# Expert pairs written out one after the other, token splits ahead of the weight splits at each joint, and twelve filler products

## What is computed

```python
def moe_swiglu(h, w_router, w_gate, w_up, w_down):
    logits = (h @ w_router).astype(jnp.float32)
    top_val, top_idx = lax.top_k(logits, TOP_K)
    top_w = jax.nn.softmax(top_val, axis=-1)
    gates = jnp.sum(jax.nn.one_hot(top_idx, N_EXPERTS, dtype=jnp.float32) * top_w[..., None], axis=-2)
    out = jnp.zeros_like(h)
    for e in range(N_EXPERTS):
        out = out + gates[..., e:e + 1] * swiglu(h, w_gate[e], w_up[e], w_down[e])
    return out
```

## Time and profile before

| | |
|---|---|
| median of 3 runs (lowest, highest) | 1273.4 us (1270.49, 1274.1) |
| the profiled execution's own time | 1276.08 us |
| its span in the profile | 1274.2 us, 16146 instructions |
| TensorE products, weight loads | busy 1221.2 us (96%), 854.6 us (67%) |
| VectorE, ScalarE, GpSimd | 689.5 us (54%), 539.2 us (42%), 106.9 us (8%) |
| mean granted TensorE clock | 0.985 of full |
| first products of the a-phases after joints 1 to 3 | at 601.01, 822.44 and 1044.35 us |
| moved by DMA | 412.58 MB, mean 324 GB/s |

### The profile page before, as it was taken

How to read it: one execution, slowest core, us unless ns; L and a number is a source line. 1 busy time by engine, 2 the same in 40 slices (tenths; PEclk the granted TensorE clock), 3 DMA queues, 4 the chain that set the end, 5 groups by cost and what they waited for, 6 DMA issues and landing times.

```text
span 1274.2 us, 16146 instructions
## 1 busy us (share of the span) xinstructions
PE 1221.2 (96%) x6044; PEld 854.6 (67%) x6044; DVE 689.5 (54%) x783; ACT 539.2 (42%) x522; POOL 106.9 (8%) x118
## 2 busy tenths in 40 slices
PE   9999999989989999998899999889999988999996
PEld 7888887778877888334688833568883346888332
DVE  3844445656578888102688710268861026886102
ACT  2643444455445776002577500257750025775001
POOL 0000000000003050100005010000501000050100
PEclk8999999999999999999999999999999999999998
DMA  9755553853266999999999999999999999999995
GB/s 314 257 187 178 196 178 120 199 188 131 100 248 225 372 363 360 347 409 414 413 415 406 368 371 408 415 414 415 407 346 386 407 415 414 415 406 341 391 407 209
DMA packets 141294, 412.58 MB, mean 324 GB/s; under 512 B 9683, under 2 KB 29139, under 8 KB 141142
## 3 DMA queue, kind: packets, MB, share of 16 engines
q1 hardware_dynamic: 140406, 408.23, 84.5%
q0 software_dynamic: 816, 3.28, 0.8%
HBM read 410.44 MB, written 1.05 MB: 323 GB/s over the span
## 4 chain that ended last, share of the span: by engine, by line
PE 85%; DMA 5%; DVE 3%; SPq 3%; issue 3%; ACT 1%; DVEq 0%; ACTq 0%
PE bank L1395 19%; PE bank L1396 19%; PE bank L1397 19%; PE bank L1768 13%; DMA raw<-in_moe_w_gate 4%; PE bank L1781 4%; SPq L545 3%; PE bank L1721 1%; PE bank L1402 1%; PE bank L1844 1%; PE bank L1491 1%; PE bank L1798 1%; PE bank L1657 1%; DMA head_row<-in_heads 1%; ACT w_hi L604 1%
## 5 line engine op out<-in xcount | busy, mean ns | idle before, releaser
L906 DVE TENSOR_TENSOR raw_lo<-raw,w_hi 128x2048 fp32r<-128x2048 f32 x149 | 339.8, 2300 | 101.4 <-ACT w_hi L604 101.2
L604 ACT ACTIVATE w_hi<-raw 128x2048 fp32r<-128x2048 f32 x149 | 284.5, 1916 | 148.3 <-PE bank L1397 95.7
L1395 PE MATMUL bank<-w_hi,h_hi 128*128 128x512 f32 x568 | 230.2, 405 | 19.4 <-DVE h_lo L1249 9.8
L1396 PE MATMUL bank<-raw_lo,h_hi 128*128 128x512 f32 x576 | 229.9, 399 | 9.1 <-issue 9.1
L1397 PE MATMUL bank<-w_hi,h_lo 128*128 128x512 f32 x568 | 226.5, 399 | 0.0
L1395 PEld LDWEIGHTS bank<-w_hi,h_hi 128*128 128x128 f32 x568 | 109.6, 193 | 50.2 <-DVE raw_lo L906 17.2
L1768 PE MATMUL bank<-raw,h_b 128*64 128x512 f32 (+1 forms) x768 | 143.1, 524 | 0.0
L1396 PEld LDWEIGHTS bank<-raw_lo,h_hi 128*128 128x128 f32 x576 | 111.1, 193 | 33.1 <-issue 10.4
L1397 PEld LDWEIGHTS bank<-w_hi,h_lo 128*128 128x128 f32 x568 | 109.2, 192 | 23.9
L906 DVE TENSOR_TENSOR raw_extra_lo<-raw_extra,w_hi 128x2048 fp32r<-128x2048 f32 x48 | 111.4, 2348 | 15.4 <-ACT w_hi L604 15.4
L1768 PEld LDWEIGHTS bank<-raw,h_b 128*64 128x64 f32 x768 | 53.7, 137 | 82.6 <-issue 74.5
(11 more groups left out here) (311 smaller groups left out, 1601.9 us busy)
## 6 DMA issues: line engine op xcount, KB each, us to landing
raw<-in_moe_w_gate SPq DMA_DIRECT2D x96, 1024.0 KB, 11.4
raw<-in_moe_w_up SPq DMA_DIRECT2D x80, 1024.0 KB, 11.8
raw<-in_moe_w_down SPq DMA_DIRECT2D x64, 1024.0 KB, 12.6
raw_extra<-in_moe_w_down SPq DMA_DIRECT2D x48, 1024.0 KB, 13.9
raw_extra<-in_moe_w_up SPq DMA_DIRECT2D x32, 1024.0 KB, 12.7
raw_extra<-in_moe_w_gate SPq DMA_DIRECT2D x16, 1024.0 KB, 7.4
raw<-in_ffn_w_gate SPq DMA_DIRECT2D x11, 1024.0 KB, 5.1
raw<-in_ffn_w_up SPq DMA_DIRECT2D x11, 1024.0 KB, 5.1
```

The source lines that it names most:

```text
L604: nc.scalar.activation(to, raw_slot(source), ACT.Copy).then_inc(hi_ready, 1)
L906: nc.vector.tensor_tensor(lo_slot(source), raw_slot(source), high.bitcast(f32), ALU.subtract).then_inc(lo_ready, 1)
L1395: mm(out, a_hi, b_hi, start=first, stop=False)
L1396: mm(out, a_hi, b_lo, start=False, stop=False)
```

## The change

1. Every engine but SyncE and GpSimd has the first four pairs written out in its program. A loop over further pairs follows, behind an `If` that skips it when there are only four. Inside the first three pairs the `If`s on the number of pairs are gone. The number of pairs is read in the fourth pair instead of before the first.
2. At the joint, `he_hi` stands ahead of `hi_e(ROUND_UNITS)` on ScalarE, and `he_lo` ahead of `lo_e(ROUND_UNITS)` on VectorE.
3. Ahead of the next expert's first unit TensorE runs twelve products of the identity with itself (`keep_warm(WARM[8])`, L1402).
4. The places `gpos` are computed by GpSimd in 13 chained steps instead of by VectorE; VectorE only copies `rank` out of PSUM for it. The order of the experts is made by VectorE after the first `aT_low` of pair 0 instead of before the pair.

```diff
-WARM = (16, 6, 10, 8, 28, 8, 8, 8)
+WARM = (16, 6, 10, 8, 28, 8, 8, 8, 12)
...
+def pair_follows(eng, p, pairs):
+
+    return nullcontext() if isinstance(p, int) and p < PAIRS - 1 else eng.If(pairs[0] > p + 1)
+
+
+def pair_count(eng, rtab_i):
+
+    return eng.value_load(rtab_i[0:1, 0:1], min_val=PAIRS, max_val=PAIRS + X_PAIRS)
...
-            sc.wait_ge(pairs_done, 1)
-            pairs = sc.value_load(rtab_i[0:1, 0:1], min_val=PAIRS, max_val=PAIRS + X_PAIRS)
-            with sc.Fori(0, pairs) as p:
+            pairs = [None]
+
+            def pair(p):
...
-                with sc.If(p < pairs - 1):
+                if is_pair(p, PAIRS - 1):
+                    sc.wait_ge(pairs_done, 1)
+                    pairs[0] = pair_count(sc, rtab_i)
+                with pair_follows(sc, p, pairs):
+                    he_hi(p, 1)
                     hi_e(ROUND_UNITS)
-                    he_hi(p, 1)
                     hi_e(ROUND_UNITS + 1)
...
+            for p in range(PAIRS):
+                pair(p)
+            with sc.If(pairs[0] > PAIRS):
+                with sc.Fori(PAIRS, pairs[0]) as p:
+                    pair(p)
...
             he_lo(0, halves=[1])
+            nc.vector.tensor_copy(rank[:, :, :], rank_ps).then_inc(rank_copied, 1)
             lo(MOE_U0 + 2)
             lo(MOE_U0 + 3)
 
-            link(nc.vector.tensor_tensor(more, incl, big, ALU.subtract))
...
-            nc.vector.reduce_sum(gpos[:, :, :], prod[:, :, :, :], AX.X).then_inc(gpos_done, 1)
...
+            def order_table():
+                nc.vector.max(order[:, :], key)
...
+                    if is_pair(p, 0) and s == 0:
+                        order_table()
...
-                with ve.If(p < pairs - 1):
+                with pair_follows(ve, p, pairs):
+                    he_lo(p, 1)
                     lo_e(ROUND_UNITS)
-                    he_lo(p, 1)
                     lo_e(ROUND_UNITS + 1)
                     lo_e(ROUND_UNITS + 2)
                     ve.wait_ge(acc_done, p * 8 + 6)
                     accumulate(p * 8 + 4)
...
-            pe.wait_ge(pairs_done, 1)
-            pairs = pe.value_load(rtab_i[0:1, 0:1], min_val=PAIRS, max_val=PAIRS + X_PAIRS)
-            with pe.Fori(0, pairs) as p:
+            pairs = [None]
+
+            def pair(p):
...
-                with pe.If(p < pairs - 1):
+                with pair_follows(pe, p, pairs):
                     pe.wait_ge(silu_done, q0 + ELEMENTWISE)
+                    keep_warm(WARM[8])
                     expert_in(p, ROUND_UNITS + j_gate(0), 0, gate_bank, range(2), p * 2 + 3)
...
+            for p in range(PAIRS):
+                pair(p)
+            with pe.If(pairs[0] > PAIRS):
+                with pe.Fori(PAIRS, pairs[0]) as p:
+                    pair(p)
...
-            po.wait_ge(gpos_done, 1)
+            base, cap, big, incl, more, shift, most = (ctab[:, i, :] for i in (4, 5, 6, 7, 8, 9, 10))
+            po.wait_ge(pairs_done, 1)
+            nc.gpsimd.tensor_tensor(more, incl, big, ALU.subtract).then_inc(pool_step, 1)
+            po.wait_ge(pool_step, 1)
...
+            po.wait_ge(pool_step, 12)
+            nc.gpsimd.tensor_tensor(gpos[:, :, :], prod[:, :, :, 0], prod[:, :, :, 1], ALU.add).then_inc(pool_step, 1)
+            po.wait_ge(pool_step, TABLE_STEPS)
```

More of the change, by code:

```diff
@@ L1 @@
-from contextlib import ExitStack
+from contextlib import ExitStack, nullcontext
 import numpy as np
@@ L53 @@
 LAST_YG = 10
-FIRST_STEPS = 9
+TABLE_STEPS = 13
+FIRST_STEPS = TABLE_STEPS + 9
 WHOLE_UNITS = 3
@@ L301, in trunk @@
         pairs_done = sem("pairs_done")
-        gpos_done = sem("gpos_done")
+        rank_copied = sem("rank_copied")
         sel_done = sem("sel_done")
@@ L1278, in _ @@
[L1278 to L1285, removed]
@@ L1294, in _ @@
[L1294 to L1299, removed]
@@ L1301, in _ @@
-            ve.wait_ge(pairs_done, 1)
-            pairs = ve.value_load(rtab_i[0:1, 0:1], min_val=PAIRS, max_val=PAIRS + X_PAIRS)
-            with ve.Fori(0, pairs) as p:
+            def order_table():
+                nc.vector.max(order[:, :], key)
+                link(nc.vector.tensor_tensor(within[:, :, :], incl[0:1, None, :].to_broadcast([1, X_PAIRS, E]),
+                                             iota[0:1, 0:X_PAIRS, None].to_broadcast([1, X_PAIRS, E]), ALU.is_le))
+                nc.vector.max_index(order_i[:, :], order[:, :], key)
+                link(nc.vector.reduce_sum(rtab[:, :], within[:, :, :], AX.X))
+                nc.vector.tensor_copy(rtab_i[:, 1:1 + PAIRS], order_i[0:1, 0:PAIRS])
+                nc.vector.tensor_scalar(rtab_i[:, 1 + PAIRS:1 + PAIRS + X_PAIRS], rtab[:, :], float(E - 1), None, ALU.min)
+                nc.vector.tensor_copy(rtab_i[:, 1 + PAIRS + X_PAIRS:1 + 2 * PAIRS + X_PAIRS],
+                                      order_i[0:1, PAIRS:2 * PAIRS]).then_inc(rtab_done, 1)
@@ L1366, in _ @@
                     accumulate(p * 8 + 4)
-                with ve.If(p < pairs - 1):
+                with pair_follows(ve, p, pairs):
                     lo_e(ROUND_UNITS + 3)
+            for p in range(PAIRS):
+                pair(p)
+            with ve.If(pairs[0] > PAIRS):
+                with ve.Fori(PAIRS, pairs[0]) as p:
+                    pair(p)
             assert yg[0] == LAST_YG
@@ L1853, in act_transposed, with old_sums @@
                     step.then_inc(aT_psum, 1)
-                for s in range(N_BG - 1):
[L1856 to L1862, removed]
+                def old_sums():
+                    pe.wait_ge(gT_done, p * 2 + 2)
+                    for tb in range(TB):
+                        for half in range(2):
+                            cols = slice(half * HALF, (half + 1) * HALF)
+                            mm(last_out(tb, half), ident, y[:, tb, cols], start=True, stop=False)
+                if is_pair(p, PAIRS - 1):
+                    pe.wait_ge(pairs_done, 1)
+                    pairs[0] = pair_count(pe, rtab_i)
+                for s in range(N_BG - 1):
+                    if s == N_BG - 2 and pairs[0] is not None:
+                        with pe.If(pairs[0] < p + 2):
+                            old_sums()
                     pe.wait_ge(silu_done, q0 + (N_EG + s + 1))
@@ L1888, in _ @@
                                start=True, stop=True).then_inc(sc_psum, 1)
-            pe.wait_ge(ye_act, pairs * 2)
-            pe.wait_ge(gT_done, pairs * 2)
+            for p in range(PAIRS):
+                pair(p)
+            with pe.If(pairs[0] > PAIRS):
+                with pe.Fori(PAIRS, pairs[0]) as p:
+                    pair(p)
+            pe.wait_ge(ye_act, pairs[0] * 2)
+            pe.wait_ge(gT_done, pairs[0] * 2)
             for tb in range(TB):
@@ new lines, in _ @@
+            nc.gpsimd.tensor_tensor(most, cap, base, ALU.add).then_inc(pool_step, 1)
+            po.wait_ge(pool_step, 3)
+            nc.gpsimd.tensor_tensor(shift, shift, most, ALU.subtract).then_inc(pool_step, 1)
+            po.wait_ge(rank_copied, 1)
+            nc.gpsimd.tensor_tensor(over[:, :, :], rank[:, :, :], cap[:, None, :].to_broadcast([P, TB, E]),
+                                    ALU.subtract).then_inc(pool_step, 1)
+            po.wait_ge(pool_step, 5)
+            nc.gpsimd.tensor_scalar(over[:, :, :], over[:, :, :], 0.0, None, ALU.is_ge).then_inc(pool_step, 1)
@@ new lines, in _ @@
+            po.wait_ge(pool_step, 9)
+            nc.gpsimd.tensor_tensor(prod[:, :, :, :], m12[:, :, :, :],
+                                    rank[:, :, None, :].to_broadcast([P, TB, 2, E]), ALU.mult).then_inc(pool_step, 1)
+            po.wait_ge(pool_step, 10)
+            nc.gpsimd.tensor_tensor(prod[:, :, :, 0:4], prod[:, :, :, 0:4], prod[:, :, :, 4:8],
+                                    ALU.add).then_inc(pool_step, 1)
+            po.wait_ge(pool_step, 11)
+            nc.gpsimd.tensor_tensor(prod[:, :, :, 0:2], prod[:, :, :, 0:2], prod[:, :, :, 2:4],
+                                    ALU.add).then_inc(pool_step, 1)
```

27 lines of the change are left out of this document (15 added, 12 removed).

## The result

The changed kernel takes 1255.1 us in the median of four runs (1254.78 to 1256.43), the kernel before 1272.7. The ratio is 0.9865 with a 95% interval from 0.9848 to 0.9882: 17.6 us or 1.35% faster. The forecast was 1251.4, the range 1244 to 1262. The profiled execution took 1256.43 us, its span is 1254.6.

The account below looks back on a forecast made before the run. The prediction saw two close bounds, the weights' stream and TensorE. Its terms, 4.1 (start of pair 0) + 19.9 (what the stream allows) - 2.0 (end) = 22.0 us, gave a median of 1251.4 us, range 1244 to 1262.

Parts of the forecast that it names:

- What bounds: In the pairs: the weights' stream and TensorE are two bounds, each a few us under the present period.
- The loop's end: At three joints: written-out pairs lose TensorE's jump gaps and slow products, 6.8 us less a new 1.1 us wait, 5.7 each.
- rival (c): At the joints: the gaps belong to fetching code, not the jump, and stay; 9.8 us gained, 1263.6 us; chance 0.08.
- Token split first, and fillers: At three joints: TensorE starts 0.2 us earlier and its clock stays up, 1.7 us; together 1.9 us each.
- What the stream allows: Periods and last stretch: the stream limits TensorE's 7.6 us a joint to 6.5, 6.5 and 6.9 us, 19.9 in all.
- Rival (b): In the pairs: the ring of 14 can't stay full, only half the stream's hole closes; 12.1 us gained, 1261.3; chance 0.11.
- Start of pair 0: Start of pair 0: without the table chain VectorE makes unit 4's low half before it is wanted; 4.1 us, passed on.
- rival (d): Pair 0: GpSimd's chain ends some 15 us late for L1791, all on TensorE; 7 us gained, 1266 us; chance 0.04.
- The end: After the last products: the `If` skips the loop body by a far jump, costing 2.0 us, between 0 and 3.5.
- Sum: Whole kernel: 22.0 us off the profiled 1276.1 gives 1254.1; the median of runs 2.7 lower, 1251.4 us.
- Rival (e): Inside the pairs: written-out code is fetched anew and TensorE stalls, 4.6 us each, two a pair giving 1288 us; chance 0.04.

Follow-up runs that it names:

- e10: The changed kernel with half of the columns of the second expert's down units not loaded, 8.3% fewer bytes: 1246.3 us, ratio 0.9789 to the kernel before.
- e1: The kernel before with the pairs written out on TensorE, VectorE and ScalarE and nothing else of the change: 1254.5 us against 1274.7, ratio 0.9849.
- e4: The kernel before with the pairs written out on TensorE alone, ScalarE and VectorE keeping their loops: 1256.1 us, ratio 0.9861 to the kernel before.
- e6: The changed kernel without its two edits at the joint (old split order, no fillers): 1254.7 us, ratio 0.9845 to the kernel before.
- e12: The changed kernel without the twelve fillers: 1252.8 us, ratio 0.9840 to the kernel before.
- e5: The changed kernel run again, unaltered: 1257.6 us, ratio 0.9876 to the kernel before.
- e3: The kernel before with only the routing table's places moved to GpSimd, the experts' order still made before the first pair: 1271.5 us against 1274.7, ratio 0.9971.
- e8: The changed kernel with the fourth unit's low half ahead of the accumulation on VectorE: 1255.9 us, ratio 0.9858 to the kernel before.
- e7: The changed kernel with TensorE's last scatter ahead of the far skip, behind a near `If`: 1252.8 us, ratio 0.9832 to the kernel before.
- e9: The changed kernel with both the last scatter ahead of the far skip and the fourth unit's low half ahead of the accumulation: 1251.3 us, ratio 0.9820.
- e2: The changed kernel with the hardware loop kept, so all of the change but the written-out pairs: 1266.7 us against 1274.7 for the kernel before, ratio 0.9944.
- e11: The kernel before with half of the columns of the second expert's down units not loaded: 1258.6 us, ratio 0.9880 to the kernel before.

## Why the prediction was right, and where it was off

**What bounds.** Right. The two bounds were there, each a few us below. e10 separates them: 214.8 us of stream, 212.5 of TensorE, where the forecast had 215 and about 213.8.

**The loop's end.** Right in mechanism: e1 and e4 show that it is TensorE's jump alone, and rival (c) is out. Too small in size: the 5.7 us a joint were 6.7 to 7.0 in e1, where the stream cut them off. The 1.1 us wait that was to come next is there, 1.04 us, at each joint.

**Token split first, and fillers.** TensorE's start and clock came out about as worked out: the first product stands 2.6 us behind the last `down_b`, for 3.1 in the forecast. But the sum let them count only through the stream's limit, and e6 shows their worth: 2.5 to 3.4 us, all up to joint 1, and nothing later. The fillers are 1.7 to 2.6 of these (e12), and 0.8 are left for the order of the splits, less than two profiles of one kernel differ by.

**What the stream allows.** 19.9 us was the term; 22.2 were measured (8.4, 6.7, 7.1), and 21.3 in the second profile of the changed kernel (e5: 7.5, 6.7, 7.1). The step that was mis-sized is "in each the smaller number decides", which took the stream's 6.5 us as the limit at joint 1 too. There the changed kernel's stream ran at 402 GB/s on average (503.52 to 716.23), below the 412 of the next stretch, and lowest at its start, behind pair 0 (301 from 503 to 520). My reading is that it had slack there and that TensorE's side came through, which was itself larger than the 7.6 of the forecast (9.0 by e10). The next stretch is right within 0.2 us or so; the third gave 7.1 where the forecast had 6.9 for the last. Cut at the first products, as the forecast did it, the excess is spread (4.9, 6.6, 7.1 and 7.4 us for 4.1, 6.5, 6.5 and 6.9), so it isn't shown that all of it belongs to joint 1. Rival (b) is out, no slice from 18 to 39 is under 405.

**Start of pair 0.** 4.1 forecast, 3.8 measured. That it passes on to the first joint holds for the kernel with the loop (e3); between e1 and e6, both written out, nothing of it arrives. GpSimd's steps took 11.7 us, within the 3 to 30; rival (d) is out.

**The end.** The term was 2.0 between 0 and 3.5; it is 3.8, 0.3 beyond the bound. Missing was the slow clock behind the idle time, 0.8 us on the way to the end. And the price is the skip's length less the distance by which the sequencer is ahead: 5.07 us less 1.7 here, of which 3.0 us reach the scatter. The forecast took the distance from the kernel before, 1.9 us, and for want of a row put the length between a near branch and 6.04 us. TensorE's sequencer waits for the last load in the changed kernel, e4, e5 and e8, and there the skip lies open; in e1, e6 and e12 it doesn't wait, and the skip is hidden; in e7 and e9 it waits, and the scatter stands ahead of the skip.

**Sum.** The pairs and the end gained 3.8 + 22.2 - 3.8 = 22.2 us, against 22.0 forecast. That this came so close is luck: the middle term was 2.3 us too small and the end 1.8 too cheap. The profiles differ by 19.65, since the changed kernel's began its pairs 2.6 us later, in a part that no edit touches; its clock up to there was 0.98, before 0.99. The medians differ by 17.6. The measured median lies 3.7 us above the forecast: 2.6 come from before the pairs, and 1.4 from the step from a profiled execution to a median, which the forecast took as 2.7 and which is 1.3 for the changed kernel. So the part before the pairs varies with the granted clock; why the clock differs there stays open. Fresh runs of the changed kernel gave 15.9 us (e5).

The parts also do not add up as the forecast had them. The written-out pairs alone gave 1254.5 us (e1), as much as the whole change; the table, the order of the splits and the fillers add nothing to them that these runs can tell.

Rival (e), code fetched anew with stalls inside the pairs, did not come: TensorE has no "issue" gap inside them, and the instruction queues together moved fewer bytes, 1.00 for 1.06 MB.

## What to carry to other kernels

TensorE's jump back at the end of a long loop body took 6 us here, with a second gap and slow products behind it, so a body run four times can pay for being written out. The far skip over what is left of the loop is better placed behind the last work that is needed (e7). Where two bounds lie 1% apart, price an edit at each place by the bound that holds there: the same edit was worth 2.5 to 3.4 us up to the first joint and nothing at the next two. Run each part of a change alone and on top of the others: the table gained in the kernel with the loop (e3) and nothing beside written-out pairs (e6). And an engine made earlier meets the next thing late, here the last load and through it the skip, so look at the end of the kernel before adding work to keep a clock warm.

## What the runs showed of the hardware

A far jump back took TensorE's sequencer 5.9 to 6.2 us (median and longest of before, e2, e3 and, with fewer bytes in the stream, e11), and a far skip 3.5 to 5.2 us at the end, when the loads ran out; a near one took 0.07 to 0.34. The far skip took 4.9 to 5.2 in the changed kernel, e5 and e8 and 3.5 to 3.9 elsewhere, in e4 too, where the last load was as late; what sets this length stays open. That the second gap of 1.9 to 3.1 us, ten products behind the jump, is code arriving late is a reading; it goes when the pairs are written out (e1), and no run separates it from the jump. The jumps back of the other engines' loops took 0.04 to 0.07 us in the trace of before.
